# Prompt attention over the memory: scores two tiles ahead of the turns, and second buffers for the probabilities

## The reference

```python
def mem_attend(q, mem_k, mem_v):
    b_, t_, _ = q.shape
    qh = q.reshape(b_, t_, XA_HEADS, XA_HD)
    s = jnp.einsum('bthd,bmhd->bhtm', qh, mem_k).astype(jnp.float32) * (XA_HD ** -0.5)
    pr = jax.nn.softmax(s, axis=-1).astype(q.dtype)
    o = jnp.einsum('bhtm,bmhd->bthd', pr, mem_v)
    return o.reshape(b_, t_, BRANCH_W)
```

```python
    xn = rmsnorm(x, norm1_g)
    proj = xn @ w_in
...
    merged = jnp.sum(gates.astype(x.dtype) * up, axis=2)
    h = x + merged @ w_out
    h = h + hier_moe(rmsnorm(h, norm2_g), rg_w, rg_b, re_w, re_b, e_wg, e_wu, e_wd)
```

## Time and profile before

| what | value |
|---|---|
| time, median of 3 runs | 1471.98 us (1471.15 to 1473.23) |
| profiled execution, own time | 1468.18 us |
| its span in the trace | 1466.4 us |
| granted TensorE clock, mean | 0.938 of full rate |
| TensorE busy | 1257.7 us (86%) |
| VectorE busy | 418.4 us (29%) |
| ScalarE busy | 326.4 us (22%) |
| bytes moved by DMA | 284.05 MB |

### The profile page before, as it was taken

The page is one execution under the profiler, slowest core; times in us unless marked ns, Lnnn a source line. Parts: engine busy times, 40 slices in busy tenths (PEclk is TensorE's granted clock), DMA queues, the critical chain, the costliest instruction groups (busy, mean ns, idle before and its releaser), DMA issues.

```text
span 1466.4 us, 25302 instructions
## 1 busy us (share of the span) xinstructions
PE 1257.7 (86%) x11318; PEld 963.1 (66%) x11318; DVE 418.4 (29%) x723; ACT 326.4 (22%) x563; POOL 96.7 (7%) x141
## 2 busy tenths in 40 slices
PE   4999999999999779999999997688888787777880
PEld 4899999979988758999999996232233322232330
DVE  5248523333352321333333334111111100110115
ACT  5453322323212321322222223000000000000001
POOL 2000000000000000000000000311111111111110
PEclk8999999998989997999999998699999999999995
DMA  7100113001213523122333547599999999999965
GB/s 211 59 29 1 34 28 122 4 5 59 87 62 87 134 76 97 44 77 76 87 87 94 177 163 281 191 393 394 413 411 411 413 412 412 412 413 411 410 275 197
DMA packets 136663, 284.05 MB, mean 194 GB/s; under 512 B 24931, under 2 KB 84533, under 8 KB 127786
## 3 DMA queue, kind: packets, MB, share of 16 engines
q1 hardware_dynamic: 130458, 270.60, 50.2%
q0 software_dynamic: 5440, 9.46, 1.7%
q10 hardware_dynamic: 656, 2.36, 0.4%
HBM read 274.11 MB, written 15.61 MB: 198 GB/s over the span
## 4 chain that ended last, share of the span: by engine, by line
PE 60%; DMA 21%; DVE 8%; SPq 5%; ACT 3%; issue 2%; POOL 2%; POOLq 0%; DVEq 0%; ACTq 0%
DMA slot<-in_e_wu_dram 12%; PE bank L1210 6%; PE bank L1212 6%; PE bank L1211 6%; DMA xg<-normed_tokens,il 6%; SPq L549 5%; PE bank L603 4%; PE bank L596 4%; PE bank L1234 3%; PE bank L1235 3%; PE bank L1236 3%; PE bank L1342 2%; PE bank L1343 2%; PE bank L1344 2%; PE bank L1786 2%
## 5 line engine op out<-in xcount | busy, mean ns | idle before, releaser
L596 PE MATMUL bank<-slot,xs 128*64 128x512 f32 x512 | 243.3, 625 | 56.7 <-DMA slot<-in_e_wu_dram 55.7
L597 PE MATMUL bank<-slot,xs 128*64 128x512 f32 x512 | 244.3, 627 | 0.0
L596 PEld LDWEIGHTS bank<-slot,xs 128*64 128x64 f32 x512 | 69.0, 143 | 196.6 <-issue 194.6
L1210 PE MATMUL bank<-xnh,wh 128*128 128x256 f32 (+1 forms) x448 | 133.9, 299 | 0.5 <-ACT bt_ogm L2081 0.5
L1211 PE MATMUL bank<-xnl,wh 128*128 128x256 f32 (+1 forms) x448 | 133.6, 298 | 0.0
L1212 PE MATMUL bank<-xnh,low 128*128 128x256 f32 (+1 forms) x448 | 133.5, 298 | 0.0
L603 PE MATMUL bank<-slot,ht 128*64 128x512 f32 x512 | 123.7, 628 | 0.5 <-DVE ht L909 0.5
L2164 DVE TENSOR_TENSOR low<-ring,wh 128x1536 fp32r<-128x1536 f32 (+1 forms) x45 | 90.1, 2006 | 105.8 <-ACT wh L1843 97.9
L793 ACT ACTIVATE sg<-bank 64x512 f32<-64x512 f32 x32 | 19.0, 594 | 414.3 <-PE bank L597 414.3
L899 DVE TENSOR_TENSOR h<-sg,bank 64x512 f32<-64x512 f32 x32 | 21.7, 679 | 313.5 <-ACT sg L793 287.8
L1210 PEld LDWEIGHTS bank<-xnh,wh 128*128 128x128 f32 x448 | 86.1, 192 | 0.7 <-ACT bt_ogm L2081 0.7
(11 more groups left out here) (474 smaller groups left out, 2602.4 us busy)
## 6 DMA issues: line engine op xcount, KB each, us to landing
slot<-in_e_wg_dram SPq DMA_DIRECT2D x64, 1024.0 KB, 20.9
slot<-in_e_wu_dram SPq DMA_DIRECT2D x64, 1024.0 KB, 21.8
slot<-in_e_wd_dram SPq DMA_DIRECT2D x64, 1024.0 KB, 19.7
ring<-in_w_in_dram SPq DMA_DIRECT2D x13, 1024.0 KB, 9.2
ring<-in_w_in_dram SPq DMA_DIRECT2D x24, 512.0 KB, 4.2
ring<-in_w_branch_dram SPq DMA_DIRECT2D x24, 256.0 KB, 4.6
kvs<-in_cache_mem_k_dram SPq DMA_DIRECT2D x8, 512.0 KB, 4.6
kvs<-in_cache_mem_v_dram SPq DMA_DIRECT2D x8, 512.0 KB, 3.6
```

The source lines that it names most:

```text
L596: pe.matmul(out[64:128, :], tok, wg[:, FF * k:FF * k + FF], start=(k == 0), stop=(k == KD - 1))
L597: mm = pe.matmul(out[0:64, :], tok, wu[:, FF * k:FF * k + FF], start=(k == 0), stop=(k == KD - 1))
L1210: pe.matmul(part, w_h, xh_(k, cols), start=(k == 0), stop=False)
```

## The change

TensorE issues the scores of tiles 0 and 1 first, then 12 filler products once. In each tile it turns the probabilities, issues the scores of the tile after next, and then the values of this tile. The 18 filler products in each of the four tiles are gone. Odd tiles have their scores in banks 6 and 7, and they have their own `prob`, `prt` and `smx`. The second `prob` and `prt` lie at `z3 + 9216`, on the memory of `qm`, so VectorE waits for the last tile's values before it clears `qm`. ScalarE takes the exponentials of tiles 0 and 1 first, and those of tile t + 2 behind tile t's output copy. VectorE normalises tile t + 1 behind its copy of turned tile t, and takes the maxima of tile t + 2 behind that. The instructions of each tile are the same as before, with the same shapes.

```diff
+        probs = [sb(f"prob{n}", [128, XH, NM], F32, at) for n, at in enumerate((z3 + 47104, z3 + 9216))]
+        prts = [sb(f"prt{n}", [128, XH * 2, 128], F32, at) for n, at in enumerate((z3 + 51200, z3 + 9216 + 4096))]
+        smxs = [sb(f"smx{n}", [128, 4, XH], F32, z3 + 55296 + 64 * n) for n in range(2)]
...
-            def score(t, t0, tn):
+            def score(t):
+                if t >= 2:
+                    act_x.wait(pe, ("p", t - 2))
                 for x in range(XH):
-                    mm = pe.matmul(psum[x // 2][0:tn, NM * (x % 2):NM * (x % 2) + NM], qt[:, x, t0:t0 + tn], ktm[:, x, :],
-                                   start=True, stop=True)
+                    mm = pe.matmul(psum[6 * (t % 2) + x // 2][:, NM * (x % 2):NM * (x % 2) + NM], qt[:, x, 128 * t:128 * t + 128],
+                                   ktm[:, x, :], start=True, stop=True)
                 pe_x.done(mm, ("score", t))
 
+            score(0)
+            score(1)
+            idle_products(pe, 5, 12)
             for t in range(4):
+                dve_x.wait(pe, ("p", t))
                 if t >= 1:
-                    act_x.wait(pe, ("p", t - 1))
-                    dve_x.wait(pe, ("max", t - 1))
-                score(t, 128 * t, 128)
-                idle_products(pe, 5, 18)
-                dve_x.wait(pe, ("p", t))
+                    dve_x.wait(pe, ("turned", t - 1))
                 for n in range(8):
...
                 pe_x.done(mm, ("turned", t))
+                if t < 2:
+                    score(t + 2)
                 act_x.wait(pe, ("turned", t))
                 dve_x.wait(pe, ("turned", t))
+                if t >= 1:
+                    act_x.wait(pe, ("o", t - 1))
...
+            exps(0, 128, 0, 0)
+            exps(1, 128, 1, 6)
             for t in range(4):
-                exps(t, 128)
                 pe_x.wait(act, ("turned", t))
-                act_x.done(act.activation(prt[:, 0:4, :], psum[2][:, :].rearrange("p (n t) -> p n t", t=128), ACT.Copy),
+                act_x.done(act.activation(prts[t % 2][:, 0:4, :], psum[2][:, :].rearrange("p (n t) -> p n t", t=128), ACT.Copy),
                            ("turned", t))
                 pe_x.wait(act, ("o", t))
                 act_x.done(act.activation(o_xa[:, :, 128 * t:128 * t + 128],
                                           psum[4][:, :].rearrange("p (x t) -> p x t", t=128), ACT.Copy), ("o", t))
+                if t < 2:
+                    exps(t + 2, 128, t % 2, 6 * (t % 2))
...
+            def tile_max(t):
+                pe_x.wait(dve, ("score", t))
+                maxima(128, ("max", t), t % 2, 6 * (t % 2))
+
+            def tile_p(t):
+                act_x.wait(dve, ("p", t))
+                normalise(128, ("p", t), t % 2)
+
+            tile_max(0)
+            tile_max(1)
+            tile_p(0)
             for t in range(4):
-                pe_x.wait(dve, ("score", t))
-                maxima(128, ("max", t))
-                act_x.wait(dve, ("p", t))
-                normalise(128, ("p", t))
                 pe_x.wait(dve, ("turned", t))
-                dve_x.done(dve.tensor_copy(prt[:, 4:8, :], psum[3][:, :].rearrange("p (n t) -> p n t", t=128)), ("turned", t))
+                dve_x.done(dve.tensor_copy(prts[t % 2][:, 4:8, :], psum[3][:, :].rearrange("p (n t) -> p n t", t=128)), ("turned", t))
+                if t < 3:
+                    tile_p(t + 1)
+                if t < 2:
+                    tile_max(t + 2)
+            pe_x.wait(dve, ("o", 3))
             seq(dve.memset(qm[:, :, :], 0.0))
```

More of the change, by code:

```diff
@@ L305, in build @@
         ktm = sb("ktm", [128, XH, NM], F32, z3 + 43008)
[L306 to L309, removed]
+        probs = [sb(f"prob{n}", [128, XH, NM], F32, at) for n, at in enumerate((z3 + 47104, z3 + 9216))]
+        prts = [sb(f"prt{n}", [128, XH * 2, 128], F32, at) for n, at in enumerate((z3 + 51200, z3 + 9216 + 4096))]
+        smxs = [sb(f"smx{n}", [128, 4, XH], F32, z3 + 55296 + 64 * n) for n in range(2)]
+        prob, prt, smx = probs[0], prts[0], smxs[0]
+        assert z3 + 55424 <= 229368
         oh = sb("oh", [128, 3 * NB, NT], F32R, z3)
@@ L498, in build @@
         pe_x = Steps(sem("pe_x"), [("mem", *x) for x in MG] + ["kt0", "kt1"]
-                     + [(w, t) for t in range(4) for w in ("score", "turned", "o")]
+                     + [("score", 0), ("score", 1)]
+                     + [x for t in range(4) for x in [("turned", t)] + ([("score", t + 2)] if t < 2 else []) + [("o", t)]]
                      + [("skt", b) for b in range(DB)] + ["sscore"] + ["sturned"])
-        act_x = Steps(sem("act_x"), [("hi", *x) for x in MG] + ["kt0", "kt1"] + [(w, t) for t in range(4) for w in ("p", "turned", "o")]
+        act_x = Steps(sem("act_x"), [("hi", *x) for x in MG] + ["kt0", "kt1", ("p", 0), ("p", 1)]
+                      + [x for t in range(4) for x in [("turned", t), ("o", t)] + ([("p", t + 2)] if t < 2 else [])]
                       + [("skt", b) for b in range(DB)] + ["sp", "sturned", "so"])
         pe_v = Steps(sem("pe_v"), [("v", b) for b in range(DB)])
-        dve_x = Steps(sem("dve_x"), [("lo", *x) for x in MG] + [(w, t) for t in range(4) for w in ("max", "p", "turned")]
+        dve_x = Steps(sem("dve_x"), [("lo", *x) for x in MG] + [("max", 0), ("max", 1), ("p", 0)]
+                      + [x for t in range(4) for x in [("turned", t)] + ([("p", t + 1)] if t < 3 else [])
+                         + ([("max", t + 2)] if t < 2 else [])]
                       + ["qm"] + [("skt", b) for b in range(DB)] + ["smax", "sp", "sturned"])
@@ L1752, in _ @@
                         mm = pe.matmul(psum[4][:, 128 * x:128 * x + 128], vn[:, m, 128 * x:128 * x + 128],
-                                       prt[:, 2 * x + m, :], start=(m == 0), stop=(m == 1))
+                                       prts[t % 2][:, 2 * x + m, :], start=(m == 0), stop=(m == 1))
                 pe_x.done(mm, ("o", t))
@@ L2124, in _ @@
                            ("skt", b))
-            exps(None, NS)
+            exps(None, NS, 0, 0)
             pe_x.wait(act, "sturned")
@@ L2488, in _, with maxima @@
                                                   psum[4 * (u % 2)][:, :].rearrange("p (m n) -> p m n", n=256)), u)
-            def maxima(tn, name):
+            def maxima(tn, name, n, bank):
                 for g in range(2):
-                    last = dve.tensor_reduce(smx[0:tn, 0, 2 * g:2 * g + 2],
-                                             psum[g][0:tn, :].rearrange("p (x n) -> p x n", n=NM), AX.X, ALU.max)
+                    last = dve.tensor_reduce(smxs[n][0:tn, 0, 2 * g:2 * g + 2],
+                                             psum[bank + g][0:tn, :].rearrange("p (x n) -> p x n", n=NM), AX.X, ALU.max)
@@ L2494, in maxima @@
                 seq(last)
[L2495 to L2500, removed]
+                dve_x.done(dve.tensor_scalar(smxs[n][0:tn, 1, :], smxs[n][0:tn, 0, :], -(128 ** -0.5), None, ALU.mult), name)
@@ new lines, in normalise @@
+            def normalise(tn, name, n):
+                seq(dve.reciprocal(smxs[n][0:tn, 3, :], smxs[n][0:tn, 2, :]))
+                dve_x.done(dve.tensor_tensor(probs[n][0:tn, :, :], probs[n][0:tn, :, :],
+                                             smxs[n][0:tn, 3, :].unsqueeze(2).to_broadcast([tn, XH, NM]), ALU.mult), name)
+            def tile_max(t):
[4 more added lines that the diff above has]
+                normalise(128, ("p", t), t % 2)
@@ L2517, in _ @@
             pe_x.wait(dve, "sscore")
-            maxima(NS, "smax")
+            maxima(NS, "smax", 0, 0)
             act_x.wait(dve, "sp")
-            normalise(NS, "sp")
+            normalise(NS, "sp", 0)
             dve_x.done(dve.tensor_copy(smx[0:NS, 0, :], smx[0:NS, 1, :]), "sturned")
```

8 lines of the change are left out of this document (4 added, 4 removed).

## The result

| | before | changed |
|---|---|---|
| median | 1471.57 us (1469.87 to 1473.23, 4 runs) | 1458.22 us (1456.57 to 1461.43, 4 runs) |
| profiled execution, own time | 1468.18 us | 1457.77 us |
| its span | 1466.4 us | 1456.0 us |
| granted clock, mean | 0.938 | 0.931 |

The median of before stands on one run more than the one above. The changed kernel is about 0.9% faster: the ratio of the times is 0.9912, with a 95% interval of 0.9891 to 0.9933, that is 9.9 to 16.0 us less. Two more sets of runs beside the experiments gave 0.9913 (0.9897 to 0.9930) and 0.9912 (0.9886 to 0.9938). The forecast was 1458.3 us, 13.7 us less.

A forecast was written before the change was run, and what follows sets the result against it. The stage was taken as bound by latency round four steps of dependent engines: 45.52 us becomes 30.38, 15.1 less; minus 1.4 for the clock, 13.7 off 1471.98 gives 1458.3 us. Likeliest case 1456.7 to 1459.9; range 1455.0 to 1463.0.

The forecast's parts named there:

- head: From the first scores to tile 0's turns at 490.50: 8.43 us, as before, with first scores 3.41 us at half rate.
- tile 0: TensorE continuous: turns 1.04, scores of tile 2 1.74, values 2.02; 4.80 us in all.
- tile 1: Values wait for ScalarE's copy behind tile 0's output copy and tile 2's exponentials; 5.29 us.
- tile 2: Turns, then values held by ScalarE's output copy, tile 3's exponentials and copy, 3.27 us with handoffs; 5.29 us.
- tile 3: Probabilities ready at 504.6, then turns 1.06, VectorE's copy 0.70, values 2.02; 3.94 us.
- exit: Last values to samples' first turn: clearing `qm` and its copies now wait for those values; 2.63 us, giving back 1.8.
- The cover: Tile 0's softmax hides the added second scores and 12 fillers, which end at about 490.2; 0.3 us thick.
- The spell behind the exit: One half-rate spell of 3.3 us as samples start, priced 1.4 us; gain 13.7 us, the forecast itself, chance 0.54.
- The shift of the values' fall: In the samples' values, the clock falling at another point costs or gives up to 1.6 us.
- a half rate beyond one spell: Sign of being wrong: half rate behind the exit lasting longer than the one spell of 3.3 us.
- The rival that the gain is taken back behind the stage: The expert stream does not start earlier: price 15 us, result 1472, chance 0.04.
- The rival of a lasting half rate through the samples: Clock stays at half rate through all eight samples: price 23.6 us, result 1482, 10 us slower, chance 0.03.

The follow-up runs named there:

- act_order: Changed kernel with tile 2's and 3's exponentials behind the copies of turned tiles 1 and 2 on ScalarE; 1460.22 us, ratio 0.9912, stage 28.67 us.
- one_prt: Changed kernel with one buffer for the turned probabilities and `qm` cleared without waiting for tile 3's values; 1455.86 us, ratio 0.9892, stage 26.36 us.
- exit_fillers: Changed kernel with 10 filler products behind the last tile's values, where TensorE waits for `qm`; 1457.82 us, ratio 0.9903, stage 28.61 us.
- one_set: Changed kernel with single buffers for probabilities and turned probabilities, `qm` cleared without waiting for tile 3's values; 1454.01 us, ratio 0.9886; again later 1455.52 us.

## Why the prediction was right

**The stage.** I laid it out at 30.38 us and it took 28.61. Of the difference of 1.77, 1.40 is the first scores: 3.41 us at half rate in the profile of before, 2.01 in that of the changed kernel and in every later one, old order included. This belongs to that one execution and not to the change, so the comparable gain of the stage is 15.5 us against the 15.1 of my sum. Part by part, predicted and measured: head 8.43 and 7.01, tile 0 4.80 and 4.63, tile 1 5.29 and 5.05, tile 2 5.29 and 5.03, tile 3 3.94 and 3.74, exit 2.63 and 3.15. ScalarE's copies held the values where I said, for 0.40 us before tile 1's and 2.12 before tile 2's (0.5 and 2.2 forecast). But act_order shows that ScalarE's order was not what bounds these tiles, as I had it: with the exponentials behind the copy the waits moved to the turns and the stage stayed. I had booked too much for its handoffs: the exponentials and the copy behind them took 2.32 us, not 2.56. At the exit I had missed that the memset starts some 0.4 us after its engine is free, as the releaser "issue" with 0.43 in the earlier trace rows says; here 0.54 us pass between the end of the values and its start (508.95 to 509.49). The turns of a tile behind the values of the last one, the long pause before tile 2's values, and the fillers and second scores that cost nothing under the first softmax came as laid out. The cover was thick enough: tile 0's turns start at 490.50 in both profiles.

**The exit.** The 1.8 us for the second buffers on `qm` were measured by one_prt as 2.25.

**The clock.** The spell behind the exit came, and exit_fillers shows that the quiet stretch brings it. Its size was off: I priced one spell of 3.3 us at 1.4, and it lasted 6.8 and cost 2.67 us (2.62 by exit_fillers). I had named a half rate beyond one spell as a sign of being wrong; 6.8 us is twice the spell that I meant, so this sign came up in part. Why it lasts twice as long as the one at 482.5 is not shown; behind that one TensorE was busy without a pause, behind this one it was not, and in one_prt, where the scores came sooner behind the fall, it lasted 3.4 us.

The evidence from which I forecast the spell was thinner than I took it to be. The fall at 482.5 stands in the profile of before alone; in the 13 later profiles the clock was 1.00 through the first scores. The waits differ a little. These are the key turns before the first scores, with TensorE's idle time before them, first in the profile of before and then in that of the changed kernel:

```profile
480.27 1.06 PE L1727 MATMUL bank<-ident,kn 128*128 128x128 f32 x8 [2.00 <-DVE vn L2487]
481.68 1.06 PE L1732 MATMUL bank<-ident,kn 128*128 128x128 f32 x8 [1.53 <-DVE vn L2501]
```

Over the 13 it is 1.40 to 1.72 us, always with 0.74 more between turns and scores. So the spell was forecast rightly from a fall that came once. The turns in the tiles ran at a granted 1.00 (the window from 486 to 511.8 us), and with fillers ahead of them so did the samples' turns. The Trainium skill says in "TensorE: Matmul & The Clock Gate", Part 4, that the full rate does not engage for transposes. The traces don't agree as far as the rate of the turns goes: 8 of them took 1.04 to 1.11 us at 1.00 and 1.95 to 1.98 at 0.50. That turns alone bring the clock down, no run here shows.

**The shift of the values' fall** cost 2.0 us in the profile, outside my 1.6 either way, and this bound was worked out wrong. I halved the 3.2 us at the full rate as I had halved the spell. But a spell is time already spent at half rate, and this is time at the full rate whose work has to be done at the other: 28 passes took 3.11 us at 1.00 (564.49 to 567.60 in the trace of before), and 101 took 21.1 at 0.50 (567.80 to 588.90), so those 28 would take 5.8, up to 2.7 us more. In exit_fillers the stretch took 26.87 us, 2.4 more than before, so some of what the spell gave back was lost there again. The range around the likeliest case had to be about 1 us wider.

**The total.** By profiles 10.4 us, by medians 13.4; the forecast of 13.7 agrees with the medians. The parts that the traces show give 10.4 as well: the stage 15.5 (comparable), less 2.67, 2.00 and 0.42. So the 3 us between the two are in no part that the two profiles show. The changed kernel's three profiles agree within 0.15 us in the stage, in the samples up to their values and in the values; what differs among them is the start of the stage, by 2.5 us, and the time behind the values, by 0.9. Of before there is one profile, and it is a fast execution: of its more than 50 runs on record two were faster than 1468.18 us. What its usual execution spends more, and in which stretch, is not shown. That the forecast lies within 0.1 us of the median is therefore partly luck. In the profiles a stage 0.4 us better stands against a spell 1.3 us dearer and a shift of 2.0 that I had taken as 0.

**What I had wrong in the argument**, though it did not show in the number, is the sentence that the fillers wait for nobody and are off the chain. That is true of the chain, and it hid their use: they held the clock. Had the change taken them out without the new order, my way of costing would have said 0 to 2 us where 15 were measured. Nor did I ask whether the second buffers were needed at all; one_prt and one_set show that they were not: 0.74 us gained in the tiles against 2.25 lost at the exit. The rival that the gain is taken back behind the stage is refuted by the expert stream, which started 9.8 us earlier for 10.4 us of gain (I had said 13 to 15). The rival of a lasting half rate through the samples fell: from 519 to 552.8 us the clock was 1.00.

## What to carry to other kernels

When a small stage goes round the engines, issue the next item's first step before this item's last ones; check in the engines' order which double buffers that needs, because TensorE's own order may already guard them, and a buffer placed on a tile that is needed next puts a wait at the exit. Filler products that hide in pauses are neither free to keep nor free to take out: in the order that shortens the pauses they land on the path (10 us here), and in the old order their removal cost 15 us through the granted clock. So look at the windows' clock beside the chain for each edit, and fill the pause that a change opens.

## What was unexpected of the hardware

- The samples' values lost the full rate within 0.5 to 3.3 us of their start and ran at 0.50 to their end, though TensorE was busy without a pause: 128 passes with 8 columns took 24.5 to 26.9 us and with 64 columns 27.1, against some 14 to 15 for as many passes at the full rate (an estimate from 28 such passes in 3.11 us, and from 36 filler passes in 4.18 us). Three fillers for every 16 passes did not change it.
- In the old order without fillers the clock fell in each of the four tiles, in or just behind a wait of 5.02 us for the softmax. The new order's tiles, with pauses up to 2.12 us, kept 1.00 in the three profiles of the changed kernel before their exit. Yet with pauses of about 1 us a spell did fall into the last tile of two kernels built on one_set (values 3.33 and 3.36 us instead of 2.04), and in one_set itself, which runs the same instructions up to there, it did not in two profiles. So the same instructions lost the full rate in two executions of four.
- The memset of `qm` began 0.43 us behind VectorE's copy before it, though the profile shows nothing that it waited for (and the same in one_prt and one_set), and 0.54 us behind the values where it did wait for them. The other handoffs on the chain were 0.02 to 0.28 us.
